# Five stage borders of a fused transformer block: stores on three queues, first operands a stage ahead, steps of an inverse moved

## The chip, the cores and the metric

The kernel runs on one core of a Trainium2 chip. The metric is the time of the device for one execution, in microseconds (us). TensorE multiplies, VectorE and ScalarE work on rows, GpSimd fills masks, makes some lower halves and issues some transfers, SyncE (SP) issues most transfers. Sixteen DMA engines carry what any of the queues issues.

## The reference

One block of a model with 512 tokens and width 2048, in float32. `x` is projected by `w_in` to 11264 columns. Eight groups of two heads go through stick-breaking attention (scores, log-sigmoid, a reversed cumulative sum as a triangular product, exponential, product with the values). Four further groups of columns go through an RWKV-7 time mix: shifts, low-rank decay, rate and gate, then a recurrence over the tokens per head. The two results are multiplied by `w_up_a` and `w_up_b`, gated by sigmoids of two more groups of columns, summed, projected by `w_o`, and normalised. Then come routing to 16384 experts by product keys, a gated side path, the experts' sum, and a last normalisation.

```python
proj = x @ w_in[i]
y_a = _stick_breaking_attention(sb_q, sb_k, sb_v) @ w_up_a[i]
y_b = _rwkv7_time_mix(rw_r, rw_k, rw_v, rw_c, ...) @ w_up_b[i]
mixed = (jax.nn.sigmoid(gate_a) * y_a + jax.nn.sigmoid(gate_b) * y_b) @ w_o[i]
x = _layer_norm(DEEPNORM_ALPHA * x + mixed, ln1_w[i], ln1_b[i])
ffn = _peer_ffn(x, peer_w_q[i], peer_sub_keys[i], peer_u[i], peer_v[i])
```

## The kernel before

The kernel is a row of stages, and each ends with a barrier of all engines, ahead of which each queue waits for its own stores to land. The stages that the change touches are the first five.

`project_in` (in the trace `a_`) turns `x`, splits it and each 256 columns of `w_in` into a high and a low half in a rounded format, and multiplies (three products for one). VectorE makes the low halves, copies every second result, and turns blocks of the expert table `peer_u` (line 123); SP stores the turned blocks in `turned_d` and the results in `proj_t`. `halves` writes the order of ScalarE and VectorE; the last steps are those with `more` false.

`rwkv_prepare` (`b_`) makes, for each of 8 groups of 128 channels, the factors of a chunked form of the recurrence. GpSimd first fills constants (`Setup`, 13 steps), then loads pieces of `w_in` for `Late`, the part of the projection that is spread over the later stages: a piece is 4 blocks of 128 by 128, ScalarE makes its upper half, VectorE (in attention: GpSimd) its lower half, TensorE multiplies. `stores(sp, m)` writes a group's results to `gate_d`, `xg_d`, `bonus_d`, `gx_d`, `gb_d` and `vk_d`, in 16 transfers or so, in runs of 256 to 512 bytes; after the last group follow `decay_d` and `cols_d`.

`attention_and_inverse` (`d_`) handles 8 pairs of heads. TensorE's order per pair: transposes of the values, scores, three pieces of `Late`, sums of one head, a piece, sums of the other, a piece, values, a piece. ScalarE's: `magnitudes`, `logs`, `round_sums` and `weights`, with the pieces' upper halves between (before the first pair it makes three of them; the ring of raw pieces has `RR` = 2). Beside it VectorE inverts 128 unit triangular 64 by 64 matrices, one for each partition, in 63 steps of a product (L794) and a sum (L797). The steps are dealt over 17 gaps between VectorE's other work by a list of costs and of rooms (`ROOM`, L1055): `upto` names for each gap the step at which it ends. GpSimd loads the matrices `gx_d`, 2 MB, and SP stores the inverse `wt_d` at the end.

`rwkv_scan` (`s_`) runs the recurrence over 8 chunks of 64 tokens. For each chunk SP loads `xg` (1 MB), `vk` (0.5 MB), `wt` (0.25 MB) and `gb` (0.5 MB) into a ring of four; between chunk 0 and 1 it loads `dec`. TensorE multiplies `xg` by `vk`, then a piece of `Late`, then the rest. VectorE first writes zeros into the state and identities into `vk`, waits for `dec`, and makes the pieces' lower halves.

`finish_and_mix` (`m_`) loads the attention output `at_d` (2 MB) and the scan's output `y_d`, splits the first, normalises the second (`centre`, `square`, `spread`, `root`, `norm` go to and fro between VectorE and ScalarE), and multiplies both by their weights in 32 units of 128 columns. The weights come in groups of two units.

Of the kernel before, what the change touches and what calls it, by code (L numbers as in the profile page):

```python
# [6 lines left out]
P = 128  # L7
T = 512
# [4 lines left out]
F32 = mybir.dt.float32  # L13
# [123 lines left out]
def project_in(nc, x, w_in, proj_t, expert_u, turned_d, xt):  # L137
# [8 lines left out]
    with ExitStack() as ctx:  # L146
# [108 lines left out]
        def halves(eng, part, copy, done):  # L255
# [23 lines left out]
            def step(q, i, s, more):  # L279
                if more:  # L280
                    part_of(q + 2, i + (s + 2) // 4, (s + 2) % 4)
                if s % 2 == odd:
# [3 lines left out]
                if odd:  # L286
                    eng.wait_ge(u_in[s % 2], i * 128 + 64 * (s // 2 + 1))
                    eng.wait_ge(u_stored[s % 2], i * 32 + 16 * (s // 2 + 1))
                    for c in range(Q):
                        turn(eng, u_turn[s % 2][:, Q * c:Q * c + Q, :], u_raw[s % 2], c).then_inc(u_turned, 1)  # L290
# [95 lines left out]
def rwkv_prepare(nc, proj_t, rwkv_mu, vecs, w_lora1, w_lora2, a_lora1, a_lora2, g_lora1, g_lora2,  # L386
                 xg_d, gx_d, gb_d, vk_d, bonus_d, gate_d, cols_d, decay_d, w_in, xt, expert_u, raw_d):
# [3 lines left out]
    with ExitStack() as ctx:  # L391
        def sb(name, shape, dt=F32):
# [40 lines left out]
            "const", "rows_in", "wl_in", "pe", "act", "dve", "st_g", "st_ar", "st_gm", "st_bkt", "st_vt", "st_bon", "st_end")}  # L433
# [27 lines left out]
        def _(pool):  # L461
            c = Setup(pool, s["const"])
# [17 lines left out]
            for i in range(late.pieces):  # L480
# [5 lines left out]
            late.finish(pool)  # L486

        def stores(sp, m):
# [18 lines left out]
            sp.wait_ge(s["act"], ac_.at(m, "v_copied"))  # L507
            for e in range(2):
                q, rest, k = (slice(64 * z, 64 * z + 64) for z in (e, 1 - e, e))
                sp.dma_start(gb_d[:, q, 1, m].rearrange("c s k -> s c k"), bkt[0:64, :, k]).then_inc(s["st_bkt"], 16)  # L510
                sp.dma_start(vk_d[:, rest, 1, m].rearrange("c s k -> s c k"), bkt[64:128, :, k]).then_inc(s["st_bkt"], 16)
                sp.dma_start(vk_d[:, rest, 0, m].rearrange("c s j -> s c j"), vt[:, :, k]).then_inc(s["st_vt"], 16)

        @block.sync
        def _(sp):
# [14 lines left out]
            for m in range(MB):  # L530
# [13 lines left out]
            sp.wait_ge(s["st_end"], 32)  # L544
# [2430 lines left out]
```

## Time and profile before

| what | value |
|---|---|
| median of 3 runs | 4482.07 us (4480.89 to 4486.58) |
| the profiled execution's own time | 4482.05 us |
| its span in the trace | 4480.3 us |
| TensorE busy | 4143.6 us (92%) |
| VectorE busy | 3219.2 us (72%) |
| ScalarE busy | 1557.8 us (35%) |
| GpSimd busy | 706.0 us (16%) |
| mean granted clock | 0.971 |
| starts of the stages: prepare, attention, scan, mixing | 650.9, 994.1, 1271.1, 1394.2 us |

The span is counted from the first to the last instruction that the profiler saw. A row of the timeline gives the start, the busy time of the instructions that it merges, the engine (a q behind it: its queue of transfers and waits), the line of the code, the operation and its tiles, and in brackets how long the engine was idle before it and what ended that. Matrix multiplications that overlap are merged, so their busy times add up to more than they take.

### The profile page before, as it was taken

What the parts mean: (1) busy time and instruction counts of PE and PEld (TensorE: products, weight loads), DVE (VectorE), ACT (ScalarE), POOL (GpSimd) and SP (SyncE); (2) the same over time, 40 slices, a digit from 0 to 9 for tenths busy, and PEclk for the clock granted to TensorE, in tenths of its full rate; (3) what the DMA queues carried; (4) which work ended last, traced back from release to release, by engine and by line L of the source; (5) the groups of instructions that cost most, each with busy time, mean ns of one, the idle gap of its engine ahead of it and who ended that gap; (6) DMA issues with size and microseconds to landing.
All of it is one profiled execution on the core that took longest, in us unless ns stands there. A gap on an engine that the chain in (4) does not pass through costs nothing. (4 is left out here: it accounts for less than half of the span.)

```text
span 4480.3 us, 62357 instructions
## 1 busy us (share of the span) xinstructions
PE 4143.6 (92%) x23580; PEld 3702.9 (83%) x23580; DVE 3219.2 (72%) x4931; ACT 1557.8 (35%) x2723; POOL 706.0 (16%) x581
## 2 busy tenths in 40 slices
PE   8999989979977999699977999999999999999995
PEld 6888865657756877587767999999999999999994
DVE  4444436767845444599195898888989999888997
ACT  2121113437623321322374333333333333333332
POOL 0000001113310100244500111111111111111110
PEclk9999999989989999799999999999999999999997
DMA  9999985876676479563458999999999999999995
GB/s 278 316 315 314 310 250 162 244 234 197 193 215 212 129 240 271 183 185 119 173 155 270 305 328 310 322 318 315 316 315 311 321 316 318 315 314 317 318 314 197
DMA packets 606859, 1180.09 MB, mean 263 GB/s; under 512 B 113912, under 2 KB 359520, under 8 KB 551552
## 3 DMA queue, kind: packets, MB, share of 16 engines
q1 hardware_dynamic: 535968, 804.25, 61.0%
q0 software_dynamic: 54224, 363.88, 21.4%
q10 hardware_dynamic: 16400, 8.39, 0.7%
q8 instruction: 169, 2.77, 0.2%
q14 instruction: 98, 0.80, 0.1%
HBM read 1006.90 MB, written 228.15 MB: 276 GB/s over the span
## 5 line engine op out<-in xcount | busy, mean ns | idle before, releaser
L102 PE MATMUL h_ps<-h_a,h_v 128*128 128x352 f32 x6144 | 1079.7, 324 | 24.5 <-DVE h_a L96 13.5
L102 PE MATMUL h_ps<-xs,h_ut 128*128 128x352 f32 x6144 | 1078.6, 324 | 18.9 <-DVE h_ut L96 18.9
L102 PEld LDWEIGHTS h_ps<-h_a,h_v 128*128 128x128 f32 x6144 | 1004.9, 189 | 32.9 <-DVE h_a L96 18.7
L102 PEld LDWEIGHTS h_ps<-xs,h_ut 128*128 128x128 f32 x6144 | 1011.0, 189 | 19.6 <-DVE h_ut L96 19.6
L102 PE MATMUL a_ps<-xt_hi,a_w 128*128 128x512 f32 x1792 | 553.1, 390 | 8.0 <-DVE a_w L96 8.0
L96 DVE TENSOR_TENSOR h_v<-h_v_raw,h_v 128x512 fp32r<-128x512 f32 x512 | 350.8, 685 | 75.8 <-ACT h_v L95 74.4
L102 PEld LDWEIGHTS a_ps<-xt_hi,a_w 128*128 128x128 f32 x1792 | 337.3, 188 | 78.3 <-issue 8.2
L95 ACT ACTIVATE h_v<-h_v_raw 128x512 fp32r<-128x512 f32 x512 | 318.4, 623 | 220.9 <-PE h_ps L102 217.7
L102 PE MATMUL a_ps<-xt_lo,a_w 128*128 128x512 f32 x896 | 349.2, 390 | 0.0
L2751 DVE SCALAR_TENSOR_TENSOR y_first<-h_rows,h_acts,y_first 128x2048 f32<-128x2048 f32 x128 | 300.3, 2346 | 0.0
L2745 DVE CUSTOM_DVE_ANT_0 h_rows<-h_rows,h_x_first 128x2048 f32<-128x2048 f32 x128 | 292.4, 2285 | 0.0
L96 DVE TENSOR_TENSOR h_ut<-h_u_raw,h_ut 128x512 fp32r<-128x512 f32 x288 | 198.2, 689 | 120.3 <-ACT h_ut L95 120.3
L2798 POOL DMA_INDIRECT h_rows<-in_peer_v,idx_first x128 | 139.7, 1091 | 688.9 <-DVE y_first L2751 474.0
L96 DVE TENSOR_TENSOR a_w<-a_raw,a_w 128x2048 fp32r<-128x2048 f32 x56 | 127.1, 2273 | 145.6 <-ACT a_w L95 77.1
L95 ACT ACTIVATE h_ut<-h_u_raw 128x512 fp32r<-128x512 f32 x288 | 178.8, 621 | 146.5 <-PE h_ps L102 87.5
L2798 POOL DMA_INDIRECT h_rows<-in_peer_u,idx_first x128 | 123.6, 965 | 629.0 <-DVE h_acts L2745 616.3
L95 ACT ACTIVATE h_a<-yt_last 128x352 fp32r<-128x352 f32 x128 | 63.8, 498 | 419.9 <-DVE yt_last L2719 416.4
L2735 DVE TENSOR_TENSOR yt<-yt,h_ps 128x352 f32<-128x352 f32 x403 | 202.1, 501 | 0.0
L102 PEld LDWEIGHTS a_ps<-xt_lo,a_w 128*128 128x128 f32 x896 | 168.7, 188 | 34.9
L2666 ACT ACTIVATE h_acts<-h_acts 128x1 f32<-128x1 f32 x160 | 31.7, 198 | 459.6 <-DVE h_acts L2745 459.6
L96 POOL TENSOR_TENSOR f_w<-f_raw,f_w 128x2048 fp32r<-128x2048 f32 (+1 forms) x35 | 153.0, 4371 | 209.2 <-ACT f_w L95 209.2
L102 PE MATMUL b_ps<-xt_hi,b_half 128*128 128x512 f32 x512 | 176.6, 415 | 7.9 <-DVE b_half L345 7.9
(367 smaller groups left out, 6426.3 us busy)
## 6 DMA issues: line engine op xcount, KB each, us to landing
h_v_raw<-in_peer_v SPq DMA_DIRECT2D x128, 1024.0 KB
h_u_raw<-turned_d SPq DMA_DIRECT2D x144, 512.0 KB
a_raw<-in_w_in SPq DMA_DIRECT2D x28, 2048.0 KB, 12.7
a_xin<-in_peer_u SPq DMA_DIRECT2D x224, 256.0 KB, 7.9
turned_d<-a_xin SPq DMA_DIRECT2D x56, 1024.0 KB, 7.0
raw_d<-in_peer_u SPq DMA_DIRECT2D x448, 128.0 KB, 3.7
h_u_raw<-raw_d SPq DMA_DIRECT2D x112, 512.0 KB
yt_last<-sums_d SPq DMA_DIRECT2D x124, 176.0 KB, 5.3
```

The costliest lines, as they stand in the source:

```text
L95: return act.activation(hi, whole, ACT.Copy).then_inc(done, 1)
L96: return dve.tensor_tensor(lo, whole, hi.bitcast(F32), ALU.subtract).then_inc(done, 1)
L102: mm = pe.matmul(out, lhs[a], rhs[b], start=(first and n == 0), stop=(last and n == 2))
L2666: act.activation(acts[:, j:j + 1], acts[:, j:j + 1], ACT.Gelu).then_inc(dot_gelu, 1)
L2735: dve.tensor_tensor(out, out, made, ALU.add).then_inc(y_added, 1)
L2745: dve.tensor_tensor_reduce(rows[r % RR][:, :], rows[r % RR][:, :], x1[few][:, :], 1.0, 0.0, ALU.mult, ALU.add, acts[:, j:j + 1]).then_inc( ...
L2751: dve.scalar_tensor_tensor(y[:, :], rows[r % RR][:, :], acts[:, j:j + 1], y[:, :], ALU.mult, ALU.add).then_inc(row_used, 1)
L2798: pool.indirect_dma_start(rows[r % RR][:, :], None, u_rows if of_u else v_rows, bass.IndirectOffsetOnAxis(ap=fetch_idx[few][:, c:c + 1], a ...
```

## The change

Nothing that is computed changes. The edits, stage by stage:

1. `project_in`: in the last steps VectorE turns its blocks of the table before it copies the last result, not behind it.
2. `rwkv_prepare`: GpSimd issues its first three loads of `w_in` ahead of its fills. At the end, the six stores of turned factors of the last group are issued by ScalarE, `decay_d` by GpSimd, `cols_d` by SP ahead of the last group's stores; and SP loads the first pair's queries, keys and values for attention there, into a tile that outlives the stage.
3. `attention_and_inverse`: the first pair needs no load. In pair 6, SP loads the scan's first `xg` and `vk` (the second into the tile that held the first queries, after the scores of pair 6), and VectorE writes the zeros of the state there. The room of the last gap goes from 16500 to 5000, which deals more of the inverse's steps to earlier gaps. SP stores the last block of `Late` last.
4. `rwkv_scan`: chunk 0 has no loads of `xg` and `vk` and no wait for them or for the zeros; GpSimd's first three loads come before its fills. At chunk 4, SP loads `at_d` into a new tile `at_raw`.
5. `finish_and_mix`: no load of `at_d`; the first group of weights is loaded in two halves; ScalarE and VectorE split five blocks of the attention output ahead of the first weight unit.

Two semaphores' scopes grow from the last stages to the whole run. The core of the diff:

```diff
@@ project_in, halves
+                turn_first = odd and not more
+                if turn_first:
+                    turn_u()
                 if s % 2 == odd:
                     eng.wait_ge(stored[s // 2], i * 16 + 16)
                     eng.wait_ge(blocks_done, q + 5)
                     copy(ob[s // 2][:, s % 2, :], ps[:, s, :]).then_inc(out_done[odd], 1)
-                if odd:
+                if odd and not turn_first:
+                    turn_u()
@@ rwkv_prepare, GpSimd
+            for i in range(late.RR):
+                late.load(pool, i)
             c = Setup(pool, s["const"])
...
             late.store(pool, LATE - 2)
+            pool.wait_ge(s["dve"], dv_.at(MB - 1, "decay_end"))
+            pool.dma_start(decay_d, dec[:, :, :]).then_inc(s["st_dec"], 16)
             late.store(pool, LATE - 1)
@@ rwkv_prepare, SP and ScalarE
+            if m < MB - 1:
+                stores_turned(sp, m)
...
+            sp.dma_start(cols_d, col[:, :, :]).then_inc(s["st_end"], 16)
+            for n in range(3):
+                sp.dma_start(qkv_first[:, n, :], pv[n * MB]).then_inc(qkv_first_in, 16)
             stores(sp, MB - 1)
-            sp.dma_start(decay_d, dec[:, :, :]).then_inc(s["st_end"], 16)
-            sp.dma_start(cols_d, col[:, :, :]).then_inc(s["st_end"], 16)
...
+            stores_turned(act, MB - 1)
@@ attention_and_inverse
-        ROOM = {"before": 2000, "between": 1500, "pair": 16500}
-        rooms = [ROOM["before"]] + [ROOM["between"], ROOM["pair"]] * NPAIR
+        ROOM = {"before": 2000, "between": 1500, "pair": 16500, "last": 5000}
+        rooms = [ROOM["before"]] + [ROOM["between"], ROOM["pair"]] * (NPAIR - 1) + [ROOM["between"], ROOM["last"]]
...
-            load(0)
             for i in range(RR):
                 late.load(sp, i)
             load(1)
...
+                if n == 0 and p == NPAIR - 2:
+                    sp.dma_start(xg_first[:, :, :, :], xg_d[0]).then_inc(scan_in, 16)
+                    sp.wait_ge(z_done[1], p + 1)
+                    for e in range(2):
+                        r = slice(64 - 64 * e, 128 - 64 * e)
+                        sp.dma_start(vk_first[r, e], vk_d[0, r]).then_inc(scan_in, 16)
...
             inverse.store(sp)
+            store(NPAIR - 1)
             late.store(sp, BLOCKS - 1)
-            store(NPAIR - 1)
+            sp.wait_ge(scan_in, 48)
...
                 rows(2 * p + 2)
+                if p == NPAIR - 2:
+                    dve.wait_ge(z_done[1], p + 1)
+                    for e in range(2):
+                        dve.memset(vk_first[64 * e:64 * e + 64, e, 0, :, :], 0.0).then_inc(zeroed, 1)
+            dve.wait_ge(zeroed, 2)
@@ rwkv_scan
+            for i in range(late.RR):
+                late.load(pool, i)
             Setup(pool, const).identity(ident)
...
-                sp.dma_start(xg[u][:, :, :, :], xg_d[c]).then_inc(x_in[u], 16)
-                for e in range(2):
-                    sp.dma_start(vk[u][rows(1 - e), e], vk_d[c, rows(1 - e)]).then_inc(x_in[u], 16)
+                if c >= 1:
+                    sp.dma_start(xg[u][:, :, :, :], xg_d[c]).then_inc(x_in[u], 16)
+                    for e in range(2):
+                        sp.dma_start(vk[u][rows(1 - e), e], vk_d[c, rows(1 - e)]).then_inc(x_in[u], 16)
...
+                if c == NC - R:
+                    for h in range(2):
+                        sp.dma_start(at_raw[:, 4 * h:4 * h + 4, :], at_d.rearrange("(h m) p t -> h p m t", h=2)[h])\
+                          .then_inc(at_in, 16)
+            sp.wait_ge(at_in, 32)
...
-            for e in range(2):
-                dve.memset(vk[0][rows(e), e, 0, :, :], 0.0).then_inc(zeroed, 1)
@@ finish_and_mix
-            load_w(0)
-            for h in range(2):
-                sp.dma_start(ga[:, 4 * h:4 * h + 4, :], at_d.rearrange("(h m) p t -> h p m t", h=2)[h])\
-                  .then_inc(at_in[h], 16)
+            for b in range(GB):
+                sp.dma_start(raw[0][:, :, b * P:(b + 1) * P], wv[0][0][:, :, b * P:(b + 1) * P])\
+                  .then_inc(first_in if b == 0 else raw_in[0], 16)
...
-            hi_part(0)
             for k in range(MB):
-                act.wait_ge(at_in[k // 4], 16)
                 split(act, nc.vector, "hi", ga[:, k, :], at2[0][:, k, :], at2[1][:, k, :], at_hi)
+                if k == 4:
+                    hi_part(0)
```

VectorE's order for the low halves in `finish_and_mix` changes in the same way.

## Rows read from the trace of the kernel before

**Rows 1.** The page's first part: busy time of the engines, share, instructions.
```profile
PE 4143.6 (92%) x23580; PEld 3702.9 (83%) x23580; DVE 3219.2 (72%) x4931; ACT 1557.8 (35%) x2723; POOL 706.0 (16%) x581
```

**Rows 2.** Timeline of the border from project to prepare.
```profile
641.46 0.69 DVE L285 COPY a_ob<-a_ps 128x512 f32<-128x512 f32 x1 [16.30 <-PE a_ps L102]
642.07 2.48 DVE L123 STREAM_TRANSPOSE a_xin<-a_xin 128x512 f32<-128x512 f32 x4
...
645.01 0.38 SPq L196 DMA_DIRECT2D proj_t<-a_ob  x1
...
650.93 0.35 SPq L516 DMA_DIRECT2D b_rows<-in_rwkv_mu  x1
...
654.95 2.48 POOL L324 DMA_DIRECT2D b_raw<-in_w_in  x3 [0.31 <-POOL b_zin L78]
...
661.80 0.79 PE L102 MATMUL b_ps<-xt_hi,b_half 128*128 128x512 f32 x1 [6.37 <-DVE b_half L345]
```

**Rows 3.** Timeline of the border from prepare to attention.
```profile
978.20 1.07 ACT L669 COPY b_vt<-b_ps 64x512 f32<-64x512 f32 x2
...
991.30 0.52 SPq L543 DMA_DIRECT2D cols_d<-b_col  x1
...
994.06 1.29 SPq L1065 DMA_DIRECT2D d_qkv<-proj_t  x3
...
1003.65 1.08 PE L1123 MATMUL d_ps<-d_made,d_qkv 128*128 128x128 f32 x4 [21.49 <-DMA d_qkv<-proj_t]
...
1009.58 0.63 ACT L338 ACTIVATE d_half<-d_raw 128x512 fp32r<-128x512 f32 x1 [3.66 <-DMA d_raw<-in_w_in]
1010.24 1.30 ACT L1194 ACTIVATE d_re<-d_ps 128x512 f32<-128x512 f32 x2
```

**Rows 4.** Windows: length, busy times by engine, granted clock, DMA share, GB/s.
```profile
980.00:982.00 2.00, 2.00 (x10) 1.41 (x8) 0.51 (x1) 0.00 (x0) 0.00 (x0) 1.00 0.07 16
...
984.00:986.00 2.00, 0.00 (x0) 0.00 (x0) 0.00 (x0) 0.00 (x0) 0.00 (x0) 1.00 0.94 234
```

**Rows 5.** Timeline of VectorE and ScalarE about attention's last pair.
```profile
1214.68 2.16 DVE L794 TENSOR_TENSOR d_prod<-d_wt,d_at 128x880 f32<-128x880 f32 x1
...
1234.76 1.49 DVE L1277 TENSOR_TENSOR d_re<-d_re,d_na 128x1280 f32<-128x1280 f32 x1 [0.89 <-ACT d_na L1203]
...
1237.28 1.31 ACT L95 ACTIVATE d_sp<-d_re 128x1280 fp32r<-128x1280 f32 x1
```

**Rows 6.** Timeline of the border from attention to scan.
```profile
1256.65 0.52 DVE L794 TENSOR_TENSOR d_prod<-d_wt,d_at 128x348 f32<-128x348 f32 x1
...
1257.06 0.59 ACT L361 COPY d_ob<-d_ps 128x512 f32<-128x512 f32 x1 [1.71 <-PE d_ps L102]
...
1261.66 0.32 SPq L775 DMA_DIRECT2D wt_d<-d_wt  x1
...
1271.09 0.33 SPq L866 DMA_DIRECT2D s_xg<-xg_d  x1
...
1279.58 1.97 PE L901 MATMUL s_ps<-s_vk,s_xg 128*64 128x64 f32 x32 [22.56 <-DMA s_vk<-vk_d]
...
1284.47 1.90 DVE L345 TENSOR_TENSOR s_half<-s_raw,s_half 128x512 fp32r<-128x512 f32 x3 [7.66 <-DMA s_dec<-decay_d]
```

**Rows 7.** Timeline of the border from scan to mixing.
```profile
1389.18 0.56 POOL L329 DMA_DIRECT2D proj_t<-s_ob  x1 [13.32 <-DVE s_ob L361]
...
1394.16 0.39 SPq L1372 DMA_DIRECT2D m_raw<-in_w_up_a  x1
...
1404.15 25.10 PE L102 MATMUL m_ps<-m_at,m_w 128*128 128x512 f32 x96 [16.00 <-DVE m_at L96]
...
1409.76 1.21 DVE L1567 TENSOR_REDUCE m_mean<-m_y 128x16 f32<-128x1024 f32 x1
...
1431.31 5.86 PE L102 MATMUL m_ps<-m_at,m_w 128*128 128x512 f32 x24 [2.05 <-DVE m_w L96]
```

**Rows 8.** A window early in the scan.
```profile
1298.00:1302.00 4.00, 1.77 (x34) 1.74 (x32) 1.12 (x2) 1.38 (x3) 1.09 (x2) 0.76 1.18 262
```

More of the change, by code:

```diff
@@ L281, in step, with turn_u @@
                     part_of(q + 2, i + (s + 2) // 4, (s + 2) % 4)
+                def turn_u():
+                    eng.wait_ge(u_in[s % 2], i * 128 + 64 * (s // 2 + 1))
+                    eng.wait_ge(u_stored[s % 2], i * 32 + 16 * (s // 2 + 1))
+                    for c in range(Q):
+                        turn(eng, u_turn[s % 2][:, Q * c:Q * c + Q, :], u_raw[s % 2], c).then_inc(u_turned, 1)
+                turn_first = odd and not more
+                if turn_first:
+                    turn_u()
                 if s % 2 == odd:
@@ L386, in rwkv_prepare @@
 def rwkv_prepare(nc, proj_t, rwkv_mu, vecs, w_lora1, w_lora2, a_lora1, a_lora2, g_lora1, g_lora2,
-                 xg_d, gx_d, gb_d, vk_d, bonus_d, gate_d, cols_d, decay_d, w_in, xt, expert_u, raw_d):
+                 xg_d, gx_d, gb_d, vk_d, bonus_d, gate_d, cols_d, decay_d, w_in, xt, expert_u, raw_d,
+                 qkv_first, qkv_first_in):
     pv = proj_t.rearrange("(b p) t -> b p t", p=P)
@@ L479, in _ @@
             assert c.n == 13
-            for i in range(late.pieces):
+            for i in range(late.RR, late.pieces):
                 late.load(pool, i)
@@ L797, in step, with rwkv_scan @@
         dve.tensor_tensor(wt[:, 0:s + 1, s + 1:L], wt[:, 0:s + 1, s + 1:L], tile, ALU.add).then_inc(row, 1)
-def rwkv_scan(nc, xg_d, gb_d, vk_d, decay_d, wt_d, y_d, proj_t, w_in, xt):
+def rwkv_scan(nc, xg_d, gb_d, vk_d, decay_d, wt_d, y_d, proj_t, w_in, xt, xg_first, vk_first, at_d, at_raw, at_in):
     R = 4
@@ L850, in _ @@
         def _(pool):
+            for i in range(late.RR):
+                late.load(pool, i)
             Setup(pool, const).identity(ident)
-            for i in range(late.pieces):
+            for i in range(late.RR, late.pieces):
                 late.load(pool, i)
@@ L988, with attention_and_inverse @@
 MASKED = -1.0e30
-def attention_and_inverse(nc, proj_t, at_d, gx_d, wt_d, w_in, xt, expert_u, raw_d):
+def attention_and_inverse(nc, proj_t, at_d, gx_d, wt_d, w_in, xt, expert_u, raw_d, qkv_first, xg_first, vk_first,
+                          scan_in, xg_d, vk_d):
     pv = proj_t.rearrange("(b p) t -> b p t", p=P)
@@ L1013, in attention_and_inverse @@
         keep_all, neg, tri, masked = (const[:, n, :] for n in range(4))
-        qkv = [sb(f"qkv{b}", [P, 3, T]) for b in range(2)]
+        qkv = [qkv_first, sb("qkv1", [P, 3, T])]
         qs = [sb(f"qs{b}", [P, T]) for b in range(2)]
@@ L1296, with finish_and_mix @@
 GATE_A, GATE_B = 7 * MB, 7 * MB + KT
-def finish_and_mix(nc, y_d, cols_d, bonus_d, gate_d, proj_t, at_d, yb2, w_up_a, w_up_b, w_o, ctx_mixed, ctx_next):
+def finish_and_mix(nc, y_d, cols_d, bonus_d, gate_d, proj_t, at_d, yb2, w_up_a, w_up_b, w_o, ctx_mixed, ctx_next, ga):
     GB, GW, G = 2, 256, D // 256
@@ L1343, in finish_and_mix @@
         turned, scaled, out, yb_hi, yb_lo = sem("turned"), sem("scaled"), sem("out"), sem("yb_hi"), sem("yb_lo")
-        at_in = [sem(f"at_in{h}") for h in range(2)]
+        first_in = sem("first_in")
         at_hi, at_lo, w_hi = sem("at_hi"), sem("at_lo"), sem("w_hi")
```

73 lines of the change are left out of this document (44 added, 29 removed).

## The prediction

> **What bounds the kernel now.** I read the page's engine totals first: TensorE is busy for 92% of the span [rows 1], so what it waits for at a few places is nearly all there is to win. Then I asked for the list of TensorE's waits over the first five stages and went to each long one in the timeline, engine by engine. Three of the four long ones sit where one stage hands over to the next: 21.49 us before attention [rows 3], 22.56 us before the scan [rows 6], 16.00 us before mixing [rows 7]; preparation has 6.37 us before its first piece of `w_in` [rows 2], behind the wait for its first transpose. Each has two parts, and the reader should split them so: the **exit** (last matmul of the old stage, last copy, last store landing, barrier) and the **entry** (first load issued, landing, rounding to high and low halves, first matmul). A barrier separates the stages, so a microsecond saved at either part moves all that follows, provided that the engine that was late is the one that was served.
>
> **Border 1, project to prepare.** Exit: VectorE sat idle 16.30 us, copied its last block at 641.46, turned for 2.48 us, and only then went both stores (1 MB and 0.5 MB), the last at 645.01; preparation began 5.9 us later, at 650.9 [rows 2]. With the turning put into the idle stretch, the 0.5 MB store goes at 642.2, 2.8 us sooner, and the turned megabyte has long landed. At the next exits a 0.25 MB store issued at 1389.18 was followed by the new stage at 1394.16, 5.0 us on [rows 7]; I take 5.3 us for 0.5 MB, so 3.4 us saved. Bounds: 2.8 us (landing as before) and 5.3 us (a 2 MB store at border 3 took 9.4 us to the next stage [rows 6], so a megabyte less is worth up to 2.5 us). I take 3.3. Entry: three weight loads of GpSimd go before its fills. They were issued from 654.95 and TensorE's first piece began at 661.80, 6.85 us on [rows 2]; issued at 650.9 they would allow it at 657.8. But the fills, on which TensorE's first transpose hangs, now come the 2.48 us of those issues later: transpose at 657.1, column copy, then the two halvings (0.63 us on ScalarE, 0.69 on VectorE), first piece at about 659.3 instead of 661.8 (counted from the old start of the stage). So 2.5 us, between 0.5 (if the fourth load, reissued only when the first half is made, sets the pace) and 2.6.
>
> **Border 2, prepare to attention.** Exit: after ScalarE's last copy (from 978.20, done at 979.3) nothing is computed that matters, yet SP issues until 991.30 plus 0.52, and attention starts at 994.06 [rows 3]. Counted by issue, six stores on ScalarE, `decay_d` on GpSimd and `cols_d` early take 8 of 14 issues off SP's tail and would save about 5.5 us. But the DMA engines are 0.94 busy in 984 to 986 and nearly so to 992, while in 980 to 982 they were at 0.07 [rows 4]. The bytes are the same; what is won is the 2 us of empty engines, and the two small issues at the end (1.3 us). I take 3.5, bounds 1.5 and 6. The Trainium skill has a rule that speaks against this edit (DMA: Bandwidth & Descriptors, Rules for kernel authors): spreading DMAs over the issuing engines brings no bandwidth, since all run on the same 16 engines, and saves only time on the sequencer. By it the sum is the one given below or a little less; by issue time alone it would be 2 us more. The trace's busy shares agree with the rule.
> Entry: the first attention operands are in SBUF. TensorE's start was 9.6 us after the stage's [rows 3]; it now waits for GpSimd's identity, 1.7 us after the stage's start, so 7.8 us at the first transposes. That is not yet the stage's gain. ScalarE, in order, must make three upper halves before the magnitudes of the first pair, and the third weight piece has a ring of two: its load follows the first lower half. In this trace it got that piece at 1009.58 and began the magnitudes at 1010.24, 16.2 us in [rows 3]. The 2 MB load of the inverse stands beside these loads and does not go away. If the first piece lands 4 us in, magnitudes start at 10.1 (6.1 us won); 7 us in, at 12.5 (3.7); at 9.5, at 14.9 (1.3). I take 4.5, bounds 1.3 and 7.8.
>
> **Attention's middle.** The last pair's room goes from 16500 to 5000; by the listed costs the steps after the last pair fall from 12 (51 to 62) to 6 (57 to 62), and the other pairs take one more step here and there, at most 2.2 us and in the last gap two more short ones and two memsets of 0.5 us, together about 1.7 us. Cover: before `add` of the last pair VectorE waited 0.89 us, and its result, ready at 1236.25, is used by ScalarE at 1237.28, 1.0 us later [rows 5]; the other pairs have more. So the cost is 0, up to 4 us if steps meet GpSimd's work: 2.16 us for a product of 880 elements beside it [rows 5], while 348 elements alone take 0.52 [rows 6], which makes 1.3 for 880 at most. SP's new wait (scores of pair 6) holds its loads as in the pairs before; the loads queued behind it are used 7 us later. Nothing. Where the cover is gone, each microsecond is one of TensorE.
>
> **Border 3, attention to scan.** Exit: the inverse now ends 5.0 us of steps (1256.65 to 1261.63) after the last rest, which ended at 1245.9, plus some 1.5 us beside GpSimd: 1252.4. Its 2 MB store, issued at 1261.66 and followed by the scan 9.4 us later, lands by about 1259 [rows 6]. Next in line is the late block: ScalarE's copy ends at 1257.65, and with the 5.0 us of the smaller store's exit [rows 7] the scan starts at 1262.6 instead of 1271.09 [rows 6]. 8.5, bounds 6.5 and 9.1. Entry: TensorE's first products start at once instead of 8.5 us in, but its first piece needs VectorE, and VectorE waited 7.66 us for `dec` until 1284.47, 13.4 us in [rows 6]. `dec` stood behind 2.25 MB, and now behind 0.75 MB with 0.75 MB of pieces beside it; at the 262 GB/s of a scan slice [rows 8] that is 6 us and some 2 us until the first bytes, 8.0 us in, and the eight identity copies, after GpSimd's delayed identity, are done at 7.4. So 5.4, bounds 3 and 7.5. The DMA engines are full in the scan (1.18 in one slice) [rows 8]; 1.5 MB less at the head keeps loads as far ahead as before, and 2 MB of `at_d` join the tail. They stand beside the last three pieces; ScalarE and VectorE have 1.5 us to spare there. I charge 0.7 us, bounds 0 and 3.
>
> **Border 4, scan to mixing.** The exit is unchanged. Before, TensorE began at 1404.15, 10 us in, and VectorE's `centre(0)` at 1409.76, 15.6 us in [rows 7]. The attention output no longer loads, the first weight unit comes as half a megabyte: units ready about 6.7 us in (3.3 us won), `centre(0)` at 9.6 (6.0 won). Which counts? After 96 matmuls TensorE waits 2.05 us for the fifth unit's halves [rows 7], which hang on the turn-taking of ScalarE and VectorE: theirs is the chain. I take 6.0, bounds 3.3 and 6.3.
>
> **Sum.** 3.3 + 2.5 + 3.5 + 4.5 + 8.5 + 5.4 + 6.0 - 0.7 = 33.0 us. The profiled execution took 4482.05 us (span 4480.3), like the median 4482.07. Predicted: 4449.
>
> **Rivals.** (a) Loads and stores are only moved: the entries of borders 2 and 3 land late behind the 2 MB and the full queues. With the lower bounds there and at exit 2 (1.3, 3, 1.5) and 3.5 at border 4, the gain is about 23 us, 4459. For it: full DMA engines; against: the bytes ahead shrink. (b) The whole of every wait goes: upper bounds at borders 2 and 3 give some 42 us, 4440. Against it: the orders above. (c) The inverse becomes attention's bound. Six lower halves of 1.8 us per pair keep GpSimd busy 10.7 us; if all of it met steps at half VectorE's rate, 5.3 us would be lost in each of eight pairs, 42 in all, less 15 of cover, and 33.0 - 27 leaves 6: 4476, no change that can be told. It decides once a gap grows by over 1.9 us; the pairs' waits speak against it. (d) Slower: the clock. After a wait of 2.2 us in the scan the granted clock averaged 0.76 for a slice [rows 8], that is partly the 1.2 GHz level, where a matmul takes twice as long. TensorE's first products now stand alone, with 4.6 us idle behind them. If more than 42 us of the scan's matmuls ran at the lower level, the kernel would be slower: 50 us of them give 4499. Against it: the clock came back within 4 us each time.
>
> **How the numbers follow.** My forecast (4440 to 4458) 0.68, (a) 0.16, (b) or more 0.08, (c) 0.05, (d) 0.03. To hold eight in ten, the range takes in most of what lies around (a) and the near edge of (b): 4438 to 4463. About 0.2%, 9 us, is what a measurement can tell from no change: faster 0.92, same 0.05, slower 0.03.
>
> **What would show it.** TensorE's idle stretches at the four borders come to about 12, 10, 6 and 13 us; SP's last store of preparation near 986; the magnitudes 10 to 13 us into attention; the `dec` wait under 1 us; `centre(0)` 10 us into mixing; pairs still 31.2 us apart. I am wrong if pairs lengthen, if the first magnitudes start over 15 us in, or if the scan's clock stays down.

## The result and the profile after

| | before | changed |
|---|---|---|
| first measurement, median | 4483.59 us (4480.89 to 4486.58, 4 runs) | 4457.98 us (4452.78 to 4460.53, 4 runs) |
| ratio | | 0.9938, 95% interval 0.9926 to 0.9950 |
| second measurement, median | 4484.70 us (15 runs) | 4453.58 us (4452.50 to 4454.71, 5 runs) |
| ratio | | 0.9929, 95% interval 0.9916 to 0.9943 |
| profiled execution, span | 4482.05, 4480.3 us | 4456.89, 4455.2 us |

The kernel became faster by 26 us in the first measurement and by 31 us in the second; 33 were predicted. The first median, 4457.98, lies in the range and 9 us above the forecast.

The engine totals of the page, changed kernel, show the same work in a shorter span (the counterpart of [rows 1]):

```profile
PE 4149.2 (93%) x23580; PEld 3708.6 (83%) x23580; DVE 3218.5 (72%) x4931; ACT 1562.2 (35%) x2723; POOL 702.4 (16%) x582
```

Border 1 in the timeline of the changed kernel, beside [rows 2]:

```profile
641.80 0.69 DVE L293 COPY a_ob<-a_ps 128x512 f32<-128x512 f32 x1 [5.72 <-PE a_ps L102]
642.57 0.38 SPq L196 DMA_DIRECT2D proj_t<-a_ob  x1
646.41 0.35 SPq L532 DMA_DIRECT2D b_rows<-in_rwkv_mu  x1
646.97 2.46 POOL L329 DMA_DIRECT2D b_raw<-in_w_in  x3 [645.42 <-POOLq L31]
...
653.21 0.43 PE L571 MATMUL b_ps<-b_ident,b_rows 104*128 104x104 f32 x1 [11.51 <-POOL b_zin L78]
655.31 0.79 PE L102 MATMUL b_ps<-xt_hi,b_half 128*128 128x512 f32 x1 [1.67 <-DVE b_half L350]
```

Preparation starts 4.6 us after the copy, not 9.5. Its first piece comes 8.9 us in, not 10.9, and what TensorE waits for is now GpSimd's last fill.

Border 2, the same view, beside [rows 3]:

```profile
976.80 1.07 ACT L687 COPY b_vt<-b_ps 64x512 f32<-64x512 f32 x2
977.91 0.68 ACTq L525 DMA_DIRECT2D gb_d<-b_wide  x1
...
985.79 2.16 SPq L516 DMA_DIRECT2D xg_d<-b_wide  x1
991.81 1.28 ACT L1273 ACT_TABLE_LOAD   x1 [13.93 <-PEq L31]
993.49 1.12 PE L1159 MATMUL d_ps<-d_made,vk_first 128*128 128x128 f32 x4 [12.72 <-POOL d_made L82]
995.44 0.61 ACT L343 ACTIVATE d_half<-d_raw 128x512 fp32r<-128x512 f32 x1
1001.92 0.23 DVE L813 TENSOR_TENSOR d_prod<-d_wt,d_at 128x63 f32<-128x63 f32 x1 [5.47 <-DMA d_at<-gx_d]
1002.39 0.63 ACT L343 ACTIVATE d_half<-d_raw 128x512 fp32r<-128x512 f32 x1 [6.33 <-DMA d_raw<-in_w_in]
1005.12 0.63 ACT L343 ACTIVATE d_half<-d_raw 128x512 fp32r<-128x512 f32 x1 [2.10 <-DMA d_raw<-in_w_in]
1005.66 1.29 ACT L1230 ACTIVATE d_re<-d_ps 128x512 f32<-128x512 f32 x2
1016.19 5.05 PE L1185 MATMUL d_ps<-d_sp,d_const 128*128 128x512 f32 x20 [5.84 <-DVE d_sp L96]
```

SP's last store goes at 985.79 and attention starts at 991.81, 15.0 us after the copy where it was 15.9. The first transposes come 1.7 us in, as worked out. ScalarE has the first piece 3.6 us in, but the second only together with the inverse's 2 MB (1001.92 and 1002.39), so that the magnitudes begin 13.9 us in. What TensorE did then is in the last two rows: 5.84 us of idle time, and 20 matmuls in 5.05 us.

Windows of the changed kernel (length, busy times, granted clock, DMA share, GB/s), beside [rows 4]:

```profile
978.00:980.00 2.00, 2.00 (x10) 1.59 (x9) 1.11 (x2) 0.00 (x0) 0.00 (x0) 1.00 0.51 143
980.00:982.00 2.00, 0.77 (x4) 0.29 (x2) 0.69 (x1) 0.00 (x0) 0.21 (x1) 1.00 0.93 193
982.00:984.00 2.00, 0.00 (x0) 0.00 (x0) 0.00 (x0) 0.00 (x0) 0.33 (x1) 0.80 0.75 153
...
998.00:1000.00 2.00, 2.00 (x15) 1.81 (x14) 0.00 (x0) 0.00 (x0) 0.00 (x0) 1.00 0.95 398
...
1014.00:1016.00 2.00, 0.00 (x0) 0.00 (x0) 1.35 (x1) 2.00 (x3) 0.70 (x1) 0.50 0.00 0
1016.00:1021.00 5.00, 4.81 (x20) 4.62 (x20) 2.17 (x3) 3.73 (x7) 1.28 (x1) 0.53 0.37 107
```

The DMA engines are no longer empty after the copy (0.51 where the share was 0.07), but the stores move only 143 to 193 GB/s in these three windows, and 188 on average until 990, while the 2 MB load with its neighbours moves 398 GB/s at a share of 0.95. The last two windows show the granted clock at its lower level, 1.2 GHz, before and during the first sums.

Border 3, timeline, beside [rows 6]:

```profile
1251.22 0.32 SPq L794 DMA_DIRECT2D wt_d<-d_wt  x1
...
1256.58 0.59 ACT L366 COPY d_ob<-d_ps 128x512 f32<-128x512 f32 x1 [1.71 <-PE d_ps L102]
1257.19 0.34 SPq L334 DMA_DIRECT2D proj_t<-d_ob  x1
1260.83 1.31 SPq L892 DMA_DIRECT2D s_wt<-wt_d  x2
...
1269.66 1.29 DVE L350 TENSOR_TENSOR s_half<-s_raw,s_half 128x512 fp32r<-128x512 f32 x2 [1.80 <-DMA s_dec<-decay_d]
1270.41 0.79 PE L102 MATMUL s_ps<-xt_hi,s_half 128*128 128x512 f32 x1 [5.86 <-DVE s_half L350]
```

The scan starts 4.3 us after the last copy instead of 14.0, and its first piece comes 9.6 us in instead of 14.1; `dec` is still what VectorE waits for. Border 4, beside [rows 7]:

```profile
1372.34 0.56 POOL L334 DMA_DIRECT2D proj_t<-s_ob  x1 [13.32 <-DVE s_ob L366]
1377.33 1.00 SPq L1428 DMA_DIRECT2D m_raw<-in_w_up_a  x2
...
1383.90 30.74 PE L102 MATMUL m_ps<-m_at,m_w 128*128 128x512 f32 x120 [12.57 <-DVE m_w L96]
1386.70 1.21 DVE L1609 TENSOR_REDUCE m_mean<-m_y 128x16 f32<-128x1024 f32 x1
```

`centre(0)` comes 9.4 us into mixing instead of 15.6.

In this one profile the borders give more than the 25 us by which the spans differ. What is missing lies between them: it took 321.5 us from the first piece of preparation to its last copy (316.4 before), and 250.9 us from the first magnitudes to the last copy of attention (246.8 before). Whether the change causes this was the first thing to try.

### The profile page after: what moved, and what is told of

Read it like the earlier page. It is cut to its first block and busy times, and to the rows that moved or that the text cites. A ratio compares the mean times of both kernels' runs of the same rounds, so it can differ in the third digit from the quotient of the medians.

```text
span 4455.2 us, 62361 instructions
## 1 busy us (share of the span) xinstructions
PE 4149.2 (93%) x23580; PEld 3708.6 (83%) x23580; DVE 3218.5 (72%) x4931; ACT 1562.2 (35%) x2723; POOL 702.4 (16%) x582
## 5 line engine op out<-in xcount | busy, mean ns | idle before, releaser
L95 ACT ACTIVATE h_v<-h_v_raw 128x512 fp32r<-128x512 f32 x512 | 319.1, 624 | 222.1 <-PE h_ps L102 218.0
```

Of the source, the lines that this page charges most:

```text
L95: return act.activation(hi, whole, ACT.Copy).then_inc(done, 1)
```

## The experiments

Ten kernels were run, each timed beside the kernel before on the same chip. What an edit won is read from milestones of the profiles, since one ratio is uncertain by about 0.13%, 6 us. The last three kernels build on each other, and two of the runs change two places at once; the milestones tell the places apart, the times don't.

**Border 1 put back in the changed kernel.** The turning goes after the copy again, the three loads after the fills.

```diff
-                turn_first = odd and not more
+                turn_first = False
...
-            for i in range(late.RR):
-                late.load(pool, i)
             c = Setup(pool, s["const"])
...
-            for i in range(late.RR, late.pieces):
+            for i in range(late.pieces):
```

> The changed kernel with border 1 put back: project's last turning after the copy, and preparation's first three weight loads after GpSimd's fills. In the changed kernel TensorE's first piece of preparation came 6.5 us earlier than before, but the last copy of preparation only 1.4 us earlier: 5.1 us were lost in between, where TensorE's waits for the bonus operand grew to 3.4 and 3.8 us and were followed by matmuls at 2.05 us instead of 1.10. Theory A (those longer waits are chance of one execution, and the border's gain is passed on): this kernel is about 6 us slower than the changed one, 4464, and inside its own preparation the stretch from the first piece to the last copy may be anything from 316 to 322 us. Theory B (preparation has a pace of its own, by the transfers that it shares, and eats the early start each time): this kernel is at most 2 us slower, about 4459, and its stretch from first piece to last copy is near the 316.4 us of the kernel before.

Measured: 4457.58 us (4455.41 to 4463.48), ratio 0.9947 (0.9934 to 0.9961). The first piece came at 662.80 (655.31 in the changed kernel), the stretch to the last copy was 319.0 us. By the median nothing was lost; by the ratios 0.9947 and 0.9938 or 0.9929, some 4 to 8 us, and the intervals overlap. The timing doesn't decide. The profile shows a stretch between the 316.4 us of the kernel before and the 321.5 of the changed one, and `centre(0)` at 1389.08, 2.4 and 4.2 us later than in the two profiles of the changed kernel.

**Border 1 alone in the kernel before**, the same edits the other way round.

> The kernel before with border 1 alone: project's last turning ahead of the copy, preparation's first three weight loads ahead of GpSimd's fills. By the profile of the changed kernel the first piece of preparation comes 6.5 us earlier. With border 1 put back in the changed kernel, the time did not rise (4457.6), though its interval spans 12 us. Theory A (the gain is passed on, and the executions scatter by more than it): 6 us faster than before, 4476, ratio 0.9987, and preparation's stretch from the first piece to the last copy lies within 316 to 322 us, as it did in the other profiles. Theory B (preparation eats it): within 1.5 us of before, ratio 0.9997 to 1, and the stretch is 321 us or more.

Measured: 4476.86 us (11 runs) beside 4484.70, ratio 0.9983 (0.9974 to 0.9992): 7.6 us faster, interval 3.6 to 11.7. Preparation began 4.61 us after the copy, its first piece came 8.91 us in (4.9 and 2.1 us won), and the stretch was 318.7 us. Theory A held; preparation doesn't eat the gain.

**The changed kernel again.**

> The changed kernel unchanged, for a second look at what scatters from one execution to the next. If the 5.1 us that preparation lost in the first profile belong to the change, its stretch from the first piece to the last copy is again 321.5 us; if they are chance, it is nearer to the 318.6 to 319.1 us of three other profiles. The same for attention from the first magnitudes to the last copy: 250.9 us in the first profile, 246.8 before. The border terms (start of each stage after the last copy, first piece after the start) should agree with the first profile within 0.7 us, since they hang on orders and loads, not on chance. Time: 4456 to 4460.

Measured: 4453.58 us. Its timeline at the same milestones:

```profile
655.01 0.79 PE L102 MATMUL b_ps<-xt_hi,b_half 128*128 128x512 f32 x1 [1.67 <-DVE b_half L350]
974.12 1.07 ACT L687 COPY b_vt<-b_ps 64x512 f32<-64x512 f32 x2
988.97 0.96 SPq L329 DMA_DIRECT2D d_raw<-in_w_in  x2
1001.99 1.28 ACT L1230 ACTIVATE d_re<-d_ps 128x512 f32<-128x512 f32 x2
1249.92 0.58 ACT L366 COPY d_ob<-d_ps 128x512 f32<-128x512 f32 x1 [1.71 <-PE d_ps L102]
...
1265.32 1.90 DVE L350 TENSOR_TENSOR s_half<-s_raw,s_half 128x512 fp32r<-128x512 f32 x3 [3.23 <-DMA s_dec<-decay_d]
```

Preparation took 319.1 us and attention 247.9, both less than in the first profile, with the same code. The border terms agreed within 0.2 us at border 1, exit 2 and border 4, but not everywhere within the 0.7 us expected: the magnitudes came 13.0 us in (13.9), the scan started 5.1 us after the last copy (4.3), and the wait for `dec` was 3.23 us (1.80).

**The kernel before again**, in a single run.

> The kernel before unchanged, for its second profile. The prediction took every term from one execution. In seven profiles with the same preparation as the changed kernel's or the old one, the stretch from the first piece to the last copy was 316.5 to 321.5 us, the middle one 319.0; the first profile of before had 316.4. If chance gave it the short one, this profile has 318 to 320, and attention from the first magnitudes to the last copy is 248 to 249.5 us instead of 246.8. If the change did lengthen both stretches, they are again within 0.7 us of 316.4 and 246.8. The border terms (start of the next stage after the last copy, magnitudes, first piece, centre after the start) agree with the first profile within 0.7 us either way.

Measured: 4489.93 us. Timeline:

```profile
663.44 0.80 PE L102 MATMUL b_ps<-xt_hi,b_half 128*128 128x512 f32 x1 [6.74 <-DVE b_half L345]
...
983.29 1.07 ACT L669 COPY b_vt<-b_ps 64x512 f32<-64x512 f32 x2
...
999.28 1.29 SPq L1065 DMA_DIRECT2D d_qkv<-proj_t  x3
...
1015.46 1.28 ACT L1194 ACTIVATE d_re<-d_ps 128x512 f32<-128x512 f32 x2
...
1265.58 0.59 ACT L361 COPY d_ob<-d_ps 128x512 f32<-128x512 f32 x1 [1.71 <-PE d_ps L102]
```

Preparation took 319.9 us and attention 250.1: the same code as in [rows 2, 3, 6], 3.5 and 3.3 us longer than there. The first profile of before had caught short ones in both stages, the first of the changed kernel long ones. The border terms came again within 0.3 us. So one execution differs from the next by nearly as much as the two first profiles did. A loss of 1 or 2 us by the change isn't excluded: the means of the two profiles are 318.2 and 320.3 us in preparation (319.3 over all seven profiles with the changed preparation), and 248.5 and 249.4 in attention.

**The room of the last pair as before.**

```diff
-        ROOM = {"before": 2000, "between": 1500, "pair": 16500, "last": 5000}
-        rooms = [ROOM["before"]] + [ROOM["between"], ROOM["pair"]] * (NPAIR - 1) + [ROOM["between"], ROOM["last"]]
+        ROOM = {"before": 2000, "between": 1500, "pair": 16500}
+        rooms = [ROOM["before"]] + [ROOM["between"], ROOM["pair"]] * NPAIR
```

> The changed kernel with the room of the last pair back at 16500, so that the inverse takes its steps as in the kernel before. Attention's stretch from the first magnitudes to the last copy was 4.1 us longer in the changed kernel than before. Theory A (the shorter room is paid for by about 1.5 us in the last pair, the rest of the 4.1 us comes from the first pair's wait for pieces and from the clock after waits): the scan starts about 8.3 us later than in the changed kernel, 4466. Rival B (all of the 4.1 us comes from steps moved into the other pairs): the scan starts 5.7 us later, 4464, and the pairs are back at their old distances. Rival C (nothing of it comes from the room): 9.8 us later, 4468.

Measured: 4464.93 us, ratio 0.9958 (0.9944 to 0.9971), beside 4453.58 and 4457.98. Timeline:

```profile
1252.78 0.59 ACT L366 COPY d_ob<-d_ps 128x512 f32<-128x512 f32 x1 [1.71 <-PE d_ps L102]
...
1256.12 0.32 SPq L794 DMA_DIRECT2D wt_d<-d_wt  x1
...
1265.37 1.31 SPq L892 DMA_DIRECT2D s_wt<-wt_d  x2
```

The scan starts 12.6 us after the last copy (4.3 and 5.1 in the changed kernel, 14.0 before), so the shorter room is worth 7.5 to 8.3 us at this exit. Attention's stretch was 249.9 us, within the scatter, and the scan started 7.3 and 9.4 us later after the first magnitudes than in the changed kernel's profiles (262.5 us, beside 255.2 and 253.1). Rival B (5.7 us), and rival (c) of the prediction with it, fall. Theory A (8.3) and rival C (9.8) are not told apart. In eleven of the twelve profiles the scan followed 9.2 to 9.6 us after the issue of the `wt_d` store (9.25 here, 9.43 before, 9.61 and 9.23 in the changed kernel; 10.3 once).

**The turned stores of the last group on SP's queue again.**

```diff
+            stores_turned(sp, MB - 1)
             sp.wait_ge(qkv_first_in, 48)
...
-            stores_turned(act, MB - 1)
```

> The changed kernel with the six stores of the turned blocks of the last group issued on SP's queue behind its own six, not on ScalarE's; the decays' store on GpSimd, the columns' early store and the early load of attention's operands stay. Theory A (after the last copy the DMA engines are nearly full, so the tail is the transfer of the bytes, and a second queue only fills the first 2 us): attention starts at most 1.5 us later after the last copy than in the changed kernel, no difference that can be told, 4458 to 4459.5. Rival B (the tail was issue time, as the prediction's sum by issue had it): six issues of 0.5 to 0.8 us come back one after the other, attention starts 3 to 4.5 us later, 4461 to 4462.5.

Measured: 4455.85 us, ratio 0.9939 (0.9925 to 0.9952). Attention started 15.6 us after the last copy, 0.6 to 0.8 us later than in the changed kernel. Theory A held: six issues more on one queue cost less than 1 us.

**The 2 MB of the inverse behind the pieces.**

```diff
-            inverse.load(pool)
             c = Setup(pool, filled)
...
             assert c.n == 6
+            pool.wait_ge(late.raw_in[1], 16)
+            inverse.load(pool)
```

> The changed kernel with the 2 MB load of the inverse issued behind GpSimd's fills and behind the landing of the second piece of weights, not first of all. In the changed kernel ScalarE had the first piece 3.6 us into attention, but waited 6.33 us for the second, which landed together with the 2 MB, and the first magnitudes began 13.85 us in. Theory A (the second piece stands behind the 2 MB on the shared DMA engines): the magnitudes begin 10 to 11.5 us in, and the kernel is 2 to 3.5 us faster than the changed one, 4454.5 to 4456; VectorE starts its steps some 5 us later and has cover for it in the first gap. Rival B (VectorE's steps, started late, push the first sum and the kernel gives it back): no difference, 4458, with a wait of ScalarE or TensorE for VectorE in the first pair. Rival C (the third piece, loaded only after the first lower half, sets the magnitudes, and now stands beside the 2 MB): magnitudes again 13 to 15 us in, 4457 to 4459.

Measured: 4459.13 us, ratio 0.9944 (0.9930 to 0.9957). Timeline:

```profile
995.50 0.63 ACT L343 ACTIVATE d_half<-d_raw 128x512 fp32r<-128x512 f32 x1 [0.16 <-DMA d_raw<-in_w_in]
996.03 0.56 POOL L790 DMA_DIRECT2D d_at<-gx_d  x1 [2.34 <-DMA d_raw<-in_w_in]
...
1007.05 0.63 ACT L343 ACTIVATE d_half<-d_raw 128x512 fp32r<-128x512 f32 x1 [10.92 <-DMA d_raw<-in_w_in]
1007.59 1.28 ACT L1231 ACTIVATE d_re<-d_ps 128x512 f32<-128x512 f32 x2
```

The stage started at 991.62. The second piece was there 3.9 us in instead of 10.6, so the 2 MB had held it. But the third, whose load SP issued at 998.00, now landed with the 2 MB, and the magnitudes began 16.0 us in, even later than expected. Rival C held: moving the load only moves the wait.

**The load split, and `dec` waited for later.** GpSimd issues the rest behind its third lower half.

```diff
+        queue.dma_start(self.at[:, 0:16, :], self.gx_d[:, 0:16, :]).then_inc(self.a_in, 16)
+    def load_rest(self, queue):
+        queue.dma_start(self.at[:, 16:L, :], self.gx_d[:, 16:L, :]).then_inc(self.rest_in, 16)
...
-            dve.wait_ge(dec_in, 16)
             for i in range(AHEAD):
                 late.lower_and_keep(dve, i)
+            dve.wait_ge(dec_in, 16)
```

> The changed kernel with two edits at two borders. In attention the inverse's 2 MB load is split: rows 0 to 15 (0.5 MB) first of all as before, rows 16 to 63 (1.5 MB) from GpSimd behind its third lower half. In the scan VectorE's wait for the decays stands behind its first three lower halves, not ahead of them. In four profiles of the changed kernel's border 2 the magnitudes began 12.9 to 13.9 us into the stage, and the second piece of weights landed with the 2 MB; with the load issued later the second piece was there at 3.9 us, but then the third landed with the 2 MB, 15.4 us in. Theory A (a piece lands late whenever the 2 MB stands beside it, and ScalarE's order hands that on to the magnitudes): the magnitudes begin 8.5 to 10.5 us in, 3 us won; rival B (the loads of the first pair, with the moves of peer_u, fill the DMA engines anyway): still 12 us or more. Scan: theory A, VectorE's first lower half follows the identity copies, first piece 7.3 to 8 us into the stage instead of 9.6, 1.8 us won; rival B, the second piece or the chunk's weights are late next and the first piece is earlier but the stage is not. Both theories A: 4453; both rivals: 4458.

Measured: 4448.96 us, ratio 0.9922 (0.9908 to 0.9935). The magnitudes began 10.3 us in (13.0 and 13.9), the first sums 20.9 us in (24.4 in the first profile), and the scan's first piece came 7.9 us in (9.6 and 11.0). Theories A held at both places.

**Magnitudes ahead of the third upper half**, besides.

```diff
-            for i in range(WR):
+            for i in range(WR - 1):
                 upper(i)
...
                 logs(p, 0)
+                if p == 0:
+                    upper(WR - 1)
```

> The kernel of the split load and the moved wait, and besides ScalarE makes the third upper half of attention behind the logarithms of the first pair's first head, no longer ahead of its magnitudes. Theory A (the magnitudes wait only for ScalarE's place in line: the scores are ready 7 us in): the magnitudes begin about 7 us into the stage, the first sums 19 us in instead of 24.4, and all later pairs are as much earlier; with the scan's 1.8 us the kernel is 7 us faster than the changed one, 4451. Rival B (TensorE's third piece is now the late one, since its upper half comes only after the logarithms): TensorE stands idle between its second and third piece and the first sums come 21 to 22 us in, 4453 to 4454. Rival C (the first pair is bound by VectorE and ScalarE further down, and the gain is given back by the second pair): pairs from the second on where they stand in the kernel with the split load alone.

Measured: 4447.65 us (4438.50 to 4453.90), ratio 0.9911 (0.9898 to 0.9925). Timeline:

```profile
994.12 0.63 ACT L343 ACTIVATE d_half<-d_raw 128x512 fp32r<-128x512 f32 x1 [1.61 <-DMA d_raw<-in_w_in]
996.31 1.30 ACT L1237 ACTIVATE d_re<-d_ps 128x512 f32<-128x512 f32 x2 [1.56 <-PE d_ps L1182]
...
1007.39 2.98 PE L1192 MATMUL d_ps<-d_sp,d_const 128*128 128x512 f32 x20 [0.25 <-DVE d_sp L96]
```

The stage started at 988.25: the magnitudes began 8.1 us in (about 7 expected), the first sums 19.1 us in instead of 24.4, with 0.25 us of idle time ahead of them. They took 2.98 us at a granted clock of 1.00, where the changed kernel took 5.05 us for the same 20 matmuls at 0.53, most of them at 1.2 GHz. The second pair began 36.2 us into the stage (38.8 with the split alone, 42.8 and 41.8 in the changed kernel), and attention's end kept it: 257.7 us after the stage's start beside 260.1. Theory A held.

**Preparation's transpose on the identity alone, its last stores by halves**, besides. The parts that set the edit:

```diff
-            pe.wait_ge(s["const"], 13)
+            pe.wait_ge(s["const"], 2)
...
+            for h in range(1 + last):
+                sp.wait_ge(s["dve"], dv_.at(m, "masked1" if last and h == 0 else "masked3"))
```

> The kernel with the split load, the moved wait and the magnitudes first, and two edits in preparation. TensorE's first transpose waits for the identity alone, not for all of GpSimd's fills; and the last group's six masked stores go as twelve, the first half as soon as its two masks are made, 2.9 us sooner. Entry, theory A (the transpose was held by the fills, and it holds ScalarE's first half): first piece 6 to 7 us into the stage instead of 8.9, 2 to 3 us won; rival B (the parameter rows, or the first weight piece, land only then): 8 us or more. Exit, theory A (the tail after the last copy is the time of the bytes at some 200 GB/s, and they can only be started sooner): attention starts 12.5 to 13.8 us after the last copy instead of 14.7 to 15.6; rival B (it is issue, of which there now is more on SP's queue): 15 us or more. Both theories A: 3.5 to 5 us faster than the kernel with the magnitudes first, ratio to before 0.990.

Measured: 4445.14 us (4439.69 to 4451.78), ratio 0.9919 (0.9905 to 0.9932). The first piece came 7.5 us in (8.9), attention started 14.1 us after the last copy. Both lie between theory and rival: TensorE now waits for the last row of parameters, and the stores, begun 2.9 us sooner, shortened the tail by 0.9 us only (14.9 in the kernel without them). The bytes again moved at less than the 398 GB/s of the load. Windows of this kernel:

```profile
976.00:978.00 2.00, 1.71 (x8) 1.04 (x6) 0.31 (x2) 0.00 (x0) 0.00 (x0) 1.00 0.79 174
...
980.00:982.00 2.00, 0.00 (x0) 0.00 (x0) 0.00 (x0) 0.00 (x0) 0.00 (x0) 1.00 1.01 270
```

Whether this kernel or the one with the magnitudes first is faster, their intervals don't say. The centres of both ratios lie below the changed kernel's two, though their intervals overlap with that of 0.9929; beside the kernel before they save 36 to 40 us.

## Why the prediction was right, and where it was off

Each term of the sum as the two profiles of either kernel give it, in us:

| term | before | changed | won | predicted |
|---|---|---|---|---|
| exit 1: last copy to next stage | 9.47, 9.46 | 4.61, 4.61 | 4.9 | 3.3 |
| entry 1: start to first piece | 10.87, 11.14 | 8.90, 8.90 | 2.1 | 2.5 |
| preparation, first piece to last copy | 316.4, 319.9 | 321.5, 319.1 | scatter | 0 |
| exit 2: last copy to next stage | 15.86, 15.99 | 15.01, 14.85 | 1.0 | 3.5 |
| entry 2: start to magnitudes | 16.18, 16.18 | 13.85, 13.02 | 2.7 | 4.5 |
| attention, magnitudes to last copy | 246.8, 250.1 | 250.9, 247.9 | scatter | 0 |
| exit 3 | 14.03, 14.05 | 4.25, 5.13 | 9.4 | 8.5 |
| entry 3 | 14.13, 14.16 | 9.58, 11.01 | 3.9 | 5.4 |
| scan, first piece to last store | 103.96, 102.77 | 101.93, 104.51 | 0.1, scatter | -0.7 |
| entry 4: start to `centre(0)` | 15.60, 15.51 | 9.37, 9.32 | 6.2 | 6.0 |

Without the two stretches marked as scatter alone they add up to 30.3 us, against 33.0 predicted and 26 and 31 measured. The mechanism was right on the whole: all seven border terms have the forecast's sign, and five are within 1.6 us of it. The two largest misses are both at border 2. That the sum is nearer than its terms is in part luck: terms that came out 3.5 us better and terms that came out 6.2 us worse cancel. No run put back the early loads of borders 3 and 4, or the halved first weights, by themselves; what they won is read from two profiles of either kernel, which agree within 0.1 us at border 4.

**Exit 2** is the step that failed: 3.5 us, taken from the 2 us of empty engines and the two small issues, came out at 1.0, below its lower bound of 1.5. Before, the first of the last stores went 2.3 us after the start of the last copy [rows 3]:

```profile
980.53 0.57 SPq L501 DMA_DIRECT2D gx_d<-b_wide  x1
```

In the changed kernel ScalarE can issue its first only when the copy is done, at 977.91, 1.1 us after the copy's start. So 1.2 us could be filled, not 2. From that first store to the next stage it then took no less than before: 13.9 and 13.8 us, beside 13.5 and 13.7. The transfer even became slower at first, 153 GB/s at a share of 0.75. From 978 to 990 the six windows carry 1128 GB/s times 2 us, 2.26 MB, at 188 GB/s on average; before, the five from 982 to 992 carry 2.04 MB at 204 GB/s. The kernel with six stores back on SP's queue divides the gain: it starts attention 15.6 us after the copy, so the sooner start on ScalarE's queue is worth 0.6 to 0.8 us, and the two small stores, with what else was moved there, 0.3 us where 1.3 was counted on. From its first store to the stage it took 13.3 us on one queue, less than the 13.9 and 13.8 us on two. The Trainium skill's rule (DMA: Bandwidth & Descriptors, Rules for kernel authors) that spreading transfers over several issuing engines brings no bandwidth is what this run shows. Whether the short runs of 256 to 512 bytes are what keeps these stores near 200 GB/s was not tried.

**Entry 2**, taken at 4.5 us between 1.3 and 7.8, measured 2.7. The prediction asked when the first piece would land, and it landed in 3.6 us, better than its best case of 4, from which it worked out magnitudes at 10.1. They came at 13.9 and 13.0. The piece that counted was the second, which came with the 2 MB: the wait was put at the wrong load. The runs show the mechanism in three steps: the load later, and the third piece is held; the load split, and 3 us are won; ScalarE's order changed, and 2 more. Besides, 0.9 us of the gain was lost behind the magnitudes (the second pair began 43.7 and 44.6 us in before, 42.8 and 41.8 after: 1.8 won): the pieces no longer fill TensorE's time up to the first sums. It idled 5.84 and 5.87 us ahead of them, where it had idled 1.91 and 3.30, and the sums took 5.05 and 4.92 us, partly at the lower clock, where they had taken 3.00 and 4.43.

**Entry 3** was 1.5 us short because `dec` landed late, and 1.4 us apart in two executions. The step "8.0 us in" was an estimate from 262 GB/s and some 2 us until the first bytes; it was 8.8 and 10.3. The first three lower halves did not need `dec`, as the kernel with the moved wait shows.

**Exit 1** won 1.6 us more: 5.3 us were assumed from SP's last store to the stage, and it took 3.8 (642.57 to 646.41). The row used for it, 5.0 us in [rows 7], was one of GpSimd's queue; the same distance there is 5.0 us again after the change.

**Exit 3** came out 0.9 us better. The prediction took 5.0 us from the late block's store to the scan, and it took 3.6 and 4.5; the inverse's store, followed by the scan after 9.6 and 9.2 us, is as late as it within a microsecond, as the prediction had them.

**Attention's middle, at nothing, and rivals (c) and (d):** from the second on the pairs stayed 31.1 to 31.3 us apart, once 31.6, where the clock didn't fall (see below). The last pair of the first profile was 1.5 us long (32.5 us to the last copy): its first sums waited 0.2 us more for VectorE, and then took 4.56 us at a granted clock of 0.63. In the second profile, with the same two memsets ahead of `add`, they took 2.99 us and the pair 31.1, as before. The scan's clock did not stay down: it was 0.50 until 1272, and 1.00 from 1276 on save for 0.87 and 0.70 between 1284 and 1292; before, it was 0.50 until 1282. **Rival (a)** named the place of the loss, border 2, and a gain of 23 us, 4459. The first median, 4457.98, is nearer to it than to the forecast, the second, 4453.58, lies half-way; the range was wide enough for both. Of what was to be seen, TensorE's idle stretches at borders 1 and 4 (11.5 and 12.6 us against 12 and 13), SP's last store (985.8) and `centre(0)` were right; the stretches at borders 2 and 3 (12.7 and 4.3 us against 10 and 6), the magnitudes (13.9, not 10 to 13) and the wait for `dec` (1.8, not under 1) were not.

**The scatter.** In attention the traces show a good part of it. TensorE waits 1.9 us ahead of the first sums of nearly every pair. In 58 such cases of the twelve profiles the sums then took 3.0 us, in 22 they took 4.02 to 4.55. One case of each, from the two profiles of the kernel before:

```profile
1020.79 3.00 PE L1149 MATMUL d_ps<-d_sp,d_const 128*128 128x512 f32 x20 [1.91 <-DVE d_sp L96]
1089.13 4.16 PE L1149 MATMUL d_ps<-d_sp,d_const 128*128 128x512 f32 x20 [1.87 <-DVE d_sp L96]
```

The granted clock was 1.00 in the first and 0.68 in the second, and a pair with slow sums takes 32.1 us or more where nearly all others take 31.0 to 31.4. The first profile of before had one such pair among eight, the second four, and a slow start in the first pair besides: that accounts for the 3.3 us between them. What stays open is what decides between the two after a wait of the same length, and what makes preparation longer in one execution than in another. Preparation has waits of about 3 us for the bonus operand, after some of which two matmuls take 2.05 us instead of 1.10; but the shortest stretch with the changed preparation (316.5 us) has them too, so they don't explain its length.

## What to carry to other kernels

- When several small loads must land before a stage can run, ask when the last of them lands, and what large load stands beside it. Here the large load, moved back, held the next small one. Loading only the part that the first steps need, and the rest once the stage ran, won 3 us.
- A wait at the head of a loop costs whenever what it waits for comes late; put it where the operand is first used, and put what the critical engine waits for ahead of work that serves only later pieces.
- An issue moved to another engine still waits for that engine's own work: ScalarE's first store here went when its copy was done, 1.1 us after the copy's start. Count the gain from that moment, and not from when the transfer engines fall idle.
- Terms read from one execution repeated within 0.3 us at most borders, within 0.8 to 1.4 us where they hang on loads that share the DMA engines, and within 2 to 4 us over the long stretches. Take a second profile of both kernels before explaining a loss between borders.

## What the runs showed of the hardware

- The same instructions took 316.4 and 319.9 us in preparation in two profiles of the kernel before, and 316.5 to 321.5 us in seven profiles with the changed preparation.
- TensorE idle for 5.84 us ran the next 20 matmuls in 5.05 us at a granted clock of 0.53 in 1016 to 1021 (mostly the 1.2 GHz level); after 0.25 us of idle time the same 20 took 2.98 us at 1.00. After a wait of 1.9 us they took 2.98 to 3.00 us in 58 cases and 4.02 to 4.55 us in 22 (at a granted clock of 0.62 to 0.71 in the six read: those of the two profiles of before and of the first of the changed kernel). An earlier start of what feeds TensorE is partly eaten in this way if it is left with nothing to do.
- The last 0.25 MB store was issued 3.6 us or more (SP's queue, border 3) and 5.0 us (GpSimd's, border 4) before the next stage started.
- Of two weight pieces of 0.25 MB issued together on SP's queue at 991.81, the first was in use 3.6 us later and the second 10.6 us later, at the end of a 2 MB load that GpSimd's queue had issued at 992.24; without that load the second took 3.9 us.
